# Hybrid decoder layer on one Trainium2 core: the first four mixed blocks split ahead in their own buffer, and the early output additions signalled tile by tile

## What is computed

```python
h = rms_norm(x, norm_mix_w)
q, k, v, z, b, a, rx, rgate = split(h @ w_in)            # w_in: 2048 x 6160
y_gdn = gated_deltanet_group(q, k, v, z, b, a, ...)      # 8 heads of 128
y_rg = rglru_group(rx, rgate, ...)                       # 8 groups of 128
x = x + concat([y_gdn, y_rg]) @ w_out                    # 2048 x 2048
h = rms_norm(x, norm_ffn_w)
for e in range(32):                                      # combine: 2 experts per token
    y += combine[:, e] * ((silu(h @ w1[e]) * (h @ w3[e])) @ w2[e])
out = rms_norm(x + y, norm_final_w)
```

## Time and profile before

| | us |
|---|---|
| median of 3 runs | 1487.13 |
| lowest, highest | 1485.99, 1487.37 |
| profiled execution, its own time | 1486.9 |
| span of the profiled execution | 1485.1 |
| PE, DVE, ACT busy (sum) | 1355.9, 611.0, 440.0 |
| heads and input projection | from about 72 to 396 |
| last heads stage with pieces 0 to 7 of `w_out` | 396 to 460 |
| pieces 8 to 15 and the router | 460 to 525 |
| experts | 525 to 1475 |

### The profile page before, as it was taken

One profiled execution on the slowest core, in us unless ns is written; L12 is line 12 of the kernel. 1 busy time (PEld: TensorE's weight loads), 2 busy tenths in 40 slices (PEclk: granted clock), 3 DMA queues, 4 the chain that ended last, 5 costly groups with the idle time before them and its releaser, 6 DMA issues.

```text
span 1485.1 us, 20383 instructions
## 1 busy us (share of the span) xinstructions
PE 1355.9 (91%) x7740; PEld 834.7 (56%) x7740; DVE 611.0 (41%) x1136; ACT 440.0 (30%) x865; POOL 64.4 (4%) x63
## 2 busy tenths in 40 slices
PE   5999999999899879899899899899899899989985
PEld 3899999999877743353343343343353344335332
DVE  5977787777755522223212222212132122221323
ACT  5465655656544511021011121111111111102102
POOL 0012221022100000000000000000000000000000
PEclk9999999999999989999999999999999999999998
DMA  7565555555544759999999999999999999999994
GB/s 199 152 156 151 146 146 148 140 150 145 188 131 153 302 220 429 427 427 428 428 426 429 429 428 429 429 427 429 429 427 429 429 428 428 429 428 417 429 427 178
DMA packets 147063, 481.62 MB, mean 324 GB/s; under 512 B 11385, under 2 KB 112978, under 8 KB 121810
## 3 DMA queue, kind: packets, MB, share of 16 engines
q1 hardware_dynamic: 147026, 481.10, 83.0%
HBM read 478.96 MB, written 2.12 MB: 324 GB/s over the span
## 4 chain that ended last, share of the span: by engine, by line
PE 67%; DMA 22%; DVE 5%; ACT 2%; issue 2%; SPq 1%; DVEq 0%; ACTq 0%
PE bank L559 66%; DMA ew<-in_expert_w_dram 22%; PE bank L562 2%; DVE w_parts L1421 1%; ACT ew L1333 1%; DMA fw<-in_norm_ffn_w_dram 0%; DVE fw L1872 0%; SPq L526 0%; ACT fw_r L1260 0%; DVE fw L1678 0%; DVE ew L1460 0%; DVE ew L1880 0%; DVE fw_r L1733 0%; DVE fw L1381 0%; ACT ew L1335 0%
## 5 line engine op out<-in xcount | busy, mean ns | idle before, releaser
L559 PE MATMUL bank<-ew,hT 128*64 128x512 f32 (+1 forms) x1568 | 464.8, 600 | 41.4 <-DMA ew<-in_expert_w_dram 34.6
L559 PEld LDWEIGHTS bank<-ew,hT 128*64 128x64 f32 (+1 forms) x1568 | 155.9, 141 | 337.3 <-issue 337.1
L559 PE MATMUL bank<-act_parts,w_parts 128*128 128x256 f32 x2304 | 308.6, 288 | 1.7 <-DVE w_parts L1421 1.7
L559 PEld LDWEIGHTS bank<-act_parts,w_parts 128*128 128x128 f32 x2304 | 285.7, 192 | 2.9 <-issue 1.4
L559 PE MATMUL bank<-ew 128*64 128x512 f32 (+2 forms) x1120 | 250.4, 577 | 6.9 <-DVE ew L1882 6.9
L559 PE MATMUL bank<-mixT,hT 128*64 128x512 f32 x512 | 225.4, 593 | 0.0
L1880 DVE SCALAR_TENSOR_TENSOR ew<-ew,bank 128x256 f32<-128x256 f32 x32 | 13.5, 421 | 454.2 <-ACT ew L1335 454.2
L559 PEld LDWEIGHTS bank<-ew 128*64 128x64 f32 (+1 forms) x1120 | 85.1, 142 | 148.7 <-issue 138.4
L1421 DVE TENSOR_TENSOR w_parts<-fw,w_parts 128x2048 fp32r<-128x2048 f32 x64 | 147.4, 2308 | 30.7 <-ACT w_parts L1024 29.5
L1350 ACT ACTIVATE ye_r<-bank 64x512 fp32r<-64x512 f32 x128 | 68.8, 585 | 281.3 <-PE bank L559 280.5
L1333 ACT ACTIVATE ew<-bank,gs 128x512 f32<-128x512 f32 x32 | 22.0, 687 | 422.3 <-PE bank L559 422.3
(11 more groups left out here) (238 smaller groups left out, 1048.4 us busy)
## 6 DMA issues: line engine op xcount, KB each, us to landing
ew<-in_expert_w_dram SPq DMA_DIRECT2D x160, 2048.0 KB, 16.5
mixT<-in_expert_w_dram SPq DMA_DIRECT2D x32, 2048.0 KB, 17.9
fw<-in_w_in_dram SPq DMA_DIRECT2D x48, 1024.0 KB, 5.9
fw<-in_w_out_dram SPq DMA_DIRECT2D x16, 1024.0 KB, 5.1
mixT<-in_x_dram SPq DMA_DIRECT2D x1, 2048.0 KB, 7.6
fw<-in_x_dram SPq DMA_DIRECT2D x1, 2048.0 KB, 10.0
out_dram<-fw SPq DMA_DIRECT2D x4, 512.0 KB, 2.7
hT<-decay_rows SPq DMA_DIRECT2D x8, 192.0 KB, 5.8
```

Of the source, the lines that this page charges most:

```text
L559: return nc.tensor.matmul(o, l, r, start=start, stop=stop, skip_group_check=True)
```

## The change

The parts of blocks 0 to 3 get a place of their own, `px`, in columns 6144 to 8191 of `fw_r`, and are made by ACT and DVE between body 6 and body 7; the loops of ACT and DVE end one turn earlier, and body 7 is written out. `mix_high` and `mix_rest` keep only blocks 8 to 11. `share` begins with 2, 3, 3, 4, 4 in place of 0, 3, 3, 5, 5. Because `px` lies where the router weights were loaded, their four loads move behind piece 10 and wait for piece 6 (`s_proj`). `junk1` moves into `hT`. `s_x2e` becomes one semaphore for each token tile, the addition of tile 0 waits for a new one, `s_we`, that the last matmul of tile 0 raises, and PE waits for tile t's addition before tile t's first matmul.

```diff
--- before.py
+++ after.py
@@ -200,6 +200,7 @@
         sqy = R1b.take(T)
         yb = R1b.take(T)
 
+        junk1 = R1b.take(P)
         xc = R2.take(T)
         gg = R2.take(T)
         sz = R2.take(T)
@@ -246,13 +247,12 @@
         x2 = fw[:, 8192:12288].rearrange("p (t d) -> p t d", t=NT)
         hn_hi = [fw_r[:, D:2 * D], fw_r[:, 2 * D:3 * D]]
         hn_lo = [misc_r[:, 0:D], fw_r[:, 0:D]]
+        px = fw_r[:, 6144:8192].rearrange("p (q k t) -> p q k t", q=2, k=4)
         wfin = fw[:, 0:D]
         rw = fw[:, 6144:6144 + KD * 36].rearrange("p (k n) -> p k n", k=KD)
         rb = fw[:, 6720:6756]
 
         R4 = Region(fw[:, 6756:8192], 1436)
-        junk1 = R4.take(P)
-        R4.at = 0
         lg = R4.take(NT, 8)
         le = R4.take(NT, NE)
         lm = R4.take(NT, NE)
@@ -309,7 +309,8 @@
         s_mixH = sem("s_mixH")
         s_mixL = sem("s_mixL")
         s_mixLP = sem("s_mixLP")
-        s_x2e = sem("s_x2e")
+        s_x2e = [sem("s_x2e0"), sem("s_x2e1")]
+        s_we = sem("s_we")
         s_wfin = sem("s_wfin")
         s_rgw = sem("s_rgw")
         s_init = sem("s_init")
@@ -511,11 +512,13 @@
                 if m == RING - 1:
                     sp.wait_ge(s_prm, 1)
                     sp.dma_start(x2, x_v).then_inc(s_x2r, 16)
+                    sp.dma_start(ffnp[:, :], norm_ffn_w[0].rearrange("(p k) -> p k", k=KD)).then_inc(s_ffnp, 16)
+                if m == 10:
+                    sp.wait_ge(s_proj, NH * 6 + 7)
                     sp.dma_start(rw[:, :, 0:NG], router_w_group[0].rearrange("(k p) n -> p k n", p=P)).then_inc(s_rw, 16)
                     sp.dma_start(rw[:, :, NG:], router_w_expert[0].rearrange("(k p) n -> p k n", p=P)).then_inc(s_rw, 16)
                     sp.dma_start(rb[:, 0:NG], router_b_group.broadcast_to([P, NG])).then_inc(s_rw, 16)
                     sp.dma_start(rb[:, NG:], router_b_expert.broadcast_to([P, NE])).then_inc(s_rw, 16)
-                    sp.dma_start(ffnp[:, :], norm_ffn_w[0].rearrange("(p k) -> p k", k=KD)).then_inc(s_ffnp, 16)
 
             def load_expert(e, piece):
                 half, which = piece // 2, piece % 2
@@ -731,12 +734,17 @@
                 w = wparts[:, m % RING].rearrange("p a (k n) -> p a k n", k=4)
                 for k in chunks:
                     for t in range(NT):
-                        a = [parts[:, q, c * 4 + k, t * P:(t + 1) * P] for q in range(2)]
+                        if first and k == 0 and m in (2, 4, 6):
+                            pe.wait_ge(s_x2e[t], m // 2)
+                        a = [px[:, q, k, t * P:(t + 1) * P] if c == 0 else parts[:, q, c * 4 + k, t * P:(t + 1) * P]
+                             for q in range(2)]
                         mm(o[t][:, :], a[0], w[:, 0, k, :], first and k == 0, False)
                         mm(o[t][:, :], a[0], w[:, 1, k, :], False, False)
                         l = mm(o[t][:, :], a[1], w[:, 0, k, :], False, last and k == 3)
                         if k == 3 and t == NT - 1:
                             l.then_inc(s_proj, 1)
+                        elif k == 3 and last and m < 8:
+                            l.then_inc(s_we, 1)
                         yield
 
             def early():
@@ -744,12 +752,10 @@
                 for m in range(8):
                     if m < 2:
                         pe.wait_ge(s_mixL, m + 1)
-                    elif m % 2 == 0:
-                        pe.wait_ge(s_x2e, m // 2)
                     yield from wo(m, bank[0:2], m % 2 == 0, m % 2 == 1)
 
             steps = early()
-            share = iter((0, 3, 3, 5, 5, 2, 3, 2, 3, 3, 3, 2, 3, 3, 3, 3, 2))
+            share = iter((2, 3, 3, 4, 4, 2, 3, 2, 3, 3, 3, 2, 3, 3, 3, 3, 2))
 
             def fill_w(n):
                 for _ in range(next(share)):
@@ -761,7 +767,8 @@
                 pass
             norms(NH - 1)
             pe.wait_ge(s_mixLP, 2)
-            pe.wait_ge(s_x2e, 4)
+            for t in range(NT):
+                pe.wait_ge(s_x2e[t], 4)
 
             def transposes(n):
 
@@ -1201,10 +1208,13 @@
                 gates(i)
 
             body(1, True)
-            with act.Fori(2, NH) as i:
+            with act.Fori(2, NH - 1) as i:
                 link.enter(i - 2, PER)
                 body(i, False)
-                link.leave(NH - 2)
+                link.leave(NH - 3)
+            act.wait_ge(s_mix, 8)
+            act.activation(px[:, 0], mixT[:, 0:4, :], ACT.Copy).then_inc(s_mixH, 1)
+            body(NH - 1, False)
 
             def high_out(m):
                 high(NH * 6 + m, m % RING, NH * 2 + m // RING + 1)
@@ -1212,8 +1222,7 @@
             def mix_high():
 
                 act.wait_ge(s_proj, NH * 6)
-                act.wait_ge(s_mix, 8)
-                for lo, hi in ((0, 4), (8, 12)):
+                for lo, hi in ((8, 12),):
                     act.activation(parts[:, 0, lo:hi, :], mixT[:, lo:hi, :], ACT.Copy).then_inc(s_mixH, 1)
 
             def mix_high_late():
@@ -1658,10 +1667,13 @@
                 rest(i * 6 + 7, 1)
 
             body(1, True)
-            with dve.Fori(2, NH) as i:
+            with dve.Fori(2, NH - 1) as i:
                 link.enter(i - 2, PER_DVE)
                 body(i, False)
-                link.leave(NH - 2)
+                link.leave(NH - 3)
+            dve.wait_ge(s_mixH, 1)
+            V.tensor_tensor(px[:, 1], mixT[:, 0:4, :], px[:, 0], ALU.subtract).then_inc(s_mixL, 1)
+            body(NH - 1, False)
 
             def rest_out(m):
                 rest(NH * 6 + m, m % RING)
@@ -1680,14 +1692,18 @@
                 l.then_inc(step, 1)
 
             def add_early(n):
-                dve.wait_ge(s_proj, NH * 6 + 2 * n + 2)
-                add_out(n, bank[0:2], s_x2e)
+                for t in range(NT):
+                    if t == 0:
+                        dve.wait_ge(s_we, n + 1)
+                    else:
+                        dve.wait_ge(s_proj, NH * 6 + 2 * n + 2)
+                    V.tensor_tensor(x2[:, t, n * 512:(n + 1) * 512], x2[:, t, n * 512:(n + 1) * 512],
+                                    bank[t][:, :], ALU.add).then_inc(s_x2e[t], 1)
 
             def between(n):
                 h = NH - 1
                 if n == 0:
                     gates(h)
-                    mix_rest(1, lambda a: a[:, 0:4, :])
                     mix_rest(2, lambda a: a[:, 8:12, :])
                 elif n == 1:
                     factors(h)
@@ -1722,7 +1738,8 @@
             rest_out(9)
             finish(NH - 1, ph[:, Q_RGN:Q_RGN + 1])
             mix_rest(5, lambda a: a.rearrange("p (a b) t -> p a b t", b=NH)[:, :, NH - 1, :])
-            dve.wait_ge(s_x2e, 4)
+            for t in range(NT):
+                dve.wait_ge(s_x2e[t], 4)
             for m in range(10, 12):
                 rest_out(m)
```

## The result

The changed kernel takes **1476.38 us** in the median of six runs (1475.99 to 1478.05), the kernel before 1486.59 in its six (1485.98 to 1488.13). The ratio is 0.9927, with a 95% interval of 0.9911 to 0.9943. Two later timings of the same kernel against the kernel before gave 0.9940 (0.9926 to 0.9953) and 0.9933 (0.9919 to 0.9946). The forecast was 1478.6, in a range from 1476.0 to 1482.5: the sign held and the time lies in the range, near its lower end. The gain was 10.2 us where the sum had 8.5, so the sum was 1.7 short.

A forecast was written before the change was run, and what follows sets the result against it. Experts were taken as paced by weight loading, their stream anchored to PE. The split ahead (5.36) and output additions (3.12) gave 8.48 us off, nothing back: 1478.6 us, range 1476.0 to 1482.5.

The forecast's parts named there:

- the clock behind the routing: At 520 to 526 us, PE waiting for routing at clock 0.50: gain or loss of 1.55 us, left out of the sum.
- The bound and the anchor: Expert stage: paced by loading its weights, its stream anchored to PE, so PE's earlier savings move it one for one.
- The split ahead: Before piece 0: parts made a body earlier remove a 3.81 us stall and 1.55 of half clock, together 5.36 us.
- What was late next: Piece 1's blocks 8 to 11: subtraction done by 400.3, at most 401.7; piece 1 begins at 404.3, covered by 2.6 us.
- Body 7: Added ACT copy and DVE subtraction between bodies 6 and 7: hidden by idle time, price 0, at most 2.4 us.
- Body 7 written out: ACT and DVE leave their loops one turn earlier for straight code: price 0, upper bound 0.97 us.
- The additions: Output additions tile by tile before pieces 2, 4, 6 and 8: 0.79, 0.64, 1.04 and 0.65 saved, 3.12 us.
- The router loads: Moved behind piece 10 on SP's queue: cost 0; at the old price piece 11 has 0.3 us slack, perhaps 1 us cost.
- Half the gain: Rival: another wait, weight splits at piece 3 or body 7's price, takes the stall's place; gain 5.5, 1481.6 us; chance 0.22.
- The clock elsewhere: Rival: clock falls elsewhere, at 520 to 526 us during the routing wait; 1477.1 to 1480.2 us, within the range.
- Nothing: Rival: expert weight stream has its own start, so PE's gain ends as longer wait for first `ew`; 1487 us; chance 0.07.
- Slower: Rival: ACT and DVE stall over 11.5 us in written-out body 7, say from late code; 1490.6 us; chance 0.05.

The follow-up runs named there:

- The delay of 12 matmuls: Changed kernel with 12 extra, unused matmuls on PE ahead of the norm products of head 7; median 1483.07 us against 1477.09 for the changed kernel.
- The half alone: Changed kernel with the output additions signalled by pairs again, leaving split ahead, new shares and moved router loads; median 1480.63 us against 1487.47 for the kernel before.
- the threefold work: Changed kernel with ACT's copy and DVE's subtraction into the new home each made three times between bodies 6 and 7; ratio 0.9952 to the kernel before.
- the variant with small matmuls: Changed kernel with 64 small unused matmuls, 28 before the rank products and 36 behind, in PE's waits for the routing; median 1476.40 us, ratio 0.9925.
- the variant with the addition first: Changed kernel with pieces 2 and 3's addition ahead of DVE's channel-group recurrence, and PE's wait before piece 8 tile by tile; median 1476.74 us, ratio 0.9927.

## Where the prediction was right, and the term that failed

The parts of the stage in which the diff works came out as forecast, each from its own cause. The term that failed lies outside it: the clock behind the routing, which stood in the sum at nothing. Place by place in the stage, from start to start (us). A wait is taken from the level or norm products ahead of it to the next products (pieces 2 and 4) or to the piece itself (6 and 8), so each row holds some work too, the same in both kernels:

| place | before | after | less | forecast |
|---|---|---|---|---|
| last gate matmuls of body 7 to the products ahead of piece 2 | 19.50 | 13.85 | 5.65 | 5.36 |
| wait before piece 2 | 2.89 | 1.84 | 1.05 | 0.79 |
| wait before piece 4 | 3.55 | 3.01 | 0.54 | 0.64 |
| wait before piece 6 | 1.53 | 0.37 | 1.16 | 1.04 |
| wait before piece 8 | 1.37 | 0.93 | 0.44 | 0.65 |
| the rest of the stage | 35.77 | 35.67 | 0.10 | 0 |
| stage | 64.61 | 55.67 | 8.94 | 8.48 |

**The bound and the anchor: right.** The expert stage kept its length, and what PE saved before it came off the end. The delay of 12 matmuls shows the same in the other direction.

**The split ahead: right in its cause, a little short.** DVE's first subtraction of the kernel before, alone, took 1.74 us and not the half of 2.88 that I took; it was done at 400.59, 0.10 before PE went on at 400.69, which bears the cause out. Of the 5.65, 4.06 is the stall, counted from start to start, where its recorded idle time was 3.81, and 1.53 the half clock behind it. The forecast named the idle time as up to 0.2 short for each stall. The half alone took 5.4 off the stage, since its four other waits had grown by 0.44 in sum. What was late next, piece 1's blocks, was not late: they were ready at 399.79 (398.03 + 1.76), and piece 1 began at 402.31.

**Body 7: right.** Price 0 of a possible 2.4. The cover was counted well enough: the threefold work broke out where the forecast put it. I had counted about 0.4 us of delay for DVE's first transpose; the row L1576 began 5.83 us after the body's gate matmuls (354.56), where it had been 5.53 before, and PE's next level product was not held up.

**Body 7 written out: right.** 45.95 us, as in the loop.

**The additions: 3.2 where the sum had 3.12.** Before piece 2 and piece 6 the wait went whole. Before piece 4 0.95 was left, where I had left 0.79, and before piece 8 0.33, where I had left 0.12; my sign of under 0.1 for every place but piece 4 didn't hold there. These two terms were set too high, the two others too low, since they were the recorded idle times and the places gave more than that.

**The router loads: right.** SP's queue of the changed kernel:

```profile
443.95 0.37 SPq L518 DMA_DIRECT2D fw<-in_router_w_group_dram  x1
444.36 1.95 SPq L519 DMA_DIRECT2D fw<-in_router_w_expert_dram  x1
...
448.26 0.42 SPq L510 DMA_DIRECT2D fw<-in_w_out_dram  x1
```

The expert router weights took 1.95 us to issue, and piece 11 went out at 448.26, 4.3 us after piece 6 was done. ACT split it at 460.25, after waiting for PE as before:

```profile
460.25 2.01 ACT L1031 ACTIVATE w_parts<-fw 128x1024 fp32r<-128x1024 f32 x2 [4.61 <-PE bank L562]
```

The upper bound of the old price would have been far off. The reason that the forecast gave, the `x2` load ahead, was about half of it: with `x2` behind them the router weights still took 3.86.

The Trainium skill's rule of 512 bytes for line rate (DMA: Bandwidth & Descriptors, section Specifications), weighed in the forecast, doesn't set the issue time here: the same rows took 8.36 us to issue behind `x2`, 3.86 behind a piece issued just before and 1.95 here.

**The term that failed: the clock behind the routing, put at nothing.** The forecast said of this stretch that "where in that stretch it falls and rises isn't tied to the kernel's order", took that as an even chance of 1.55 us of gain or loss, and left it out of the sum. Measured, the gather took 7.52 and 7.53 before, and 6.78, 7.11 and 6.79 after: 0.4 to 0.75 us, 0.6 in the mean, went with the change. The chance wasn't even, and 1.55 was the wrong size. In all the kernels here whose gather began at half clock it took between 6.76 and 7.55 us, so that the kernel before, at 7.52, had 0.8 to win and next to nothing to lose. That the clock makes the difference is shown by the variant with small matmuls. Why the kernel before stood at the long end isn't known: two to three profiles of each kernel don't tell an effect of the change from luck, and the variant with the addition first, 1.9 us shorter still in the stage, was back at 7.55. This part of the gain wasn't foreseen and is not to be counted on.

With it the places give 8.9 + 0.6 = 9.5 us, and the three comparisons of medians gave 10.2, 10.1 and 9.4. So about 1 us of the 1.7 that the sum lacked is placed: 0.4 in the stage, mostly idle times recorded too short, and 0.6 in the gather. The rest, 0.7, isn't placed; it is within the scatter of the start and of the expert stage, and the median of the kernel before itself moved between 1486.44 and 1487.47.

**The rivals.** Half the gain: no new wait appeared in the stage. The clock elsewhere: true, and for the better. Nothing: refuted by the delay. Slower: PE's body 7 kept its 45.95 us.

## What to carry to other kernels

A stall of the matmul engine can cost more than its idle time: read the clock of the matmuls behind it, count from start to start, and put both into the sum. Where a later stretch starts at half clock, ask also at which end of its own spread the kernel before stands. Work moved ahead costs nothing as long as it fits the idle time of the engines it is put on, in front of the very instruction that the busy engine asks for next; look for that instruction and count up to it. When two producers are signalled as a pair, look whether the consumer could start on the first; the gain is the length of one, unless the producer's own order holds the pair back, and then moving it in that order is worth more.

## What the runs showed of the hardware that I had not expected

**The clock and where a stretch begins.** The gather of 40 matmuls took 5.16 us with the clock at 1.00, and between 6.76 and 7.55 when it began at 0.50. The length follows no plain order of the place: gathers that began between 515.7 and 516.3 us took 6.78 and 6.79, at 516.7 7.11, at 517.1 6.99, at 518.9 and 519.9 6.77 and 6.76, at 521.1 7.27 and 7.51, at 525.2 to 526.5 7.45 to 7.53, and at 514.4 7.55. Nor did the clock rise a fixed time after the gather's start: a gather that began at 514.43 and one that began at 516.23 had their first matmuls of `misc_r` at full speed (0.28 us in place of 0.41) at 519.99 and 520.09. So in these profiles 0.8 us lies between kernels for this stretch, and up to 0.33 between profiles of one.

**Small matmuls hold the clock.** With 64 matmuls of 128x256 in bf16, 0.11 us each, in waits of 3.7 and 4.7 us, the clock stayed at 1.00, though 0.53 and 0.83 us of the waits were left idle. Without them it had fallen to 0.50 by the end of the waits (window from 510.75, above). Whether fewer would do wasn't tried.

**DVE beside POOL.** An operation of DVE on 128x256 took 0.96 us (L1503 at 352.94 in the changed kernel, above), while POOL was at work, and in the kernel with the threefold copy, where it came later, 0.41; the subtraction of 128x1024 took 1.41 and 1.23. POOL's timeline in the changed kernel:

```profile
345.92 7.69 POOL L1953 TENSOR_TENSOR hT<-ew,cst 128x256 f32<-128x256 f32 x6 [38.32 <-DVE ew L1549]
353.57 0.91 POOL L1960 TENSOR_TENSOR hT<-hT,cst 128x256 f32<-128x256 f32 x1
```

Two more rows of DVE from that time, one with an input from PSUM (`bank`), and the second gate operation:

```profile
347.59 0.44 DVE L1559 SCALAR_TENSOR_TENSOR ew<-bank,wk,ew 128x256 f32<-128x256 f32 x1
...
353.81 0.82 DVE L1505 TENSOR_SCALAR misc<-misc,ph 128x256 f32<-128x256 f32 x1
```

and DVE's in the kernel with the threefold copy, where POOL is done at 353.4 (subtraction, then the two gate operations):

```profile
356.41 1.23 DVE L1683 TENSOR_TENSOR fw_r<-mixT,fw_r 128x1024 fp32r<-128x1024 f32 x1
357.55 0.41 DVE L1508 SCALAR_TENSOR_TENSOR misc<-misc,ye 128x256 f32<-128x256 f32 x1
357.89 0.34 DVE L1510 TENSOR_SCALAR misc<-misc,ph 128x256 f32<-128x256 f32 x1
```

So this work of DVE is dearer beside POOL's masks than elsewhere: of the first gate operation 0.55 us of 0.96 came on top, of the second 0.48 of 0.82. The operation that reads one of its two tiles from PSUM took 0.44 beside POOL, so not every operation of DVE is slowed.

The Trainium skill (GPSIMD Engine Reference, section Specifications) says that GpSimd shares its SBUF interfaces with VectorE, and that they contend where an instruction of DVE has two inputs in SBUF. The subtraction and the first gate operation here have two such inputs, and the trace agrees, with 0.96 against 0.41 us, and with 0.44 where one input is in PSUM. The second gate operation has one tile and one column of `ph` as inputs and was slowed as well; whether that falls under the page's sentence, no run shows. No run varies POOL's work alone.
